# A transformer block with an expert-choice router: logits turned ahead of the shift, lists of maxima copied by ScalarE, second expert's down weights loaded in the router's block

## The reference, cut to what matters

```python
def expert_choice_ffn(h, w_router, w_gate, w_up, w_down):   # h: 1 x 1024 x 1024
    cap = CAPACITY * N // N_EXPERTS                          # 2 * 1024 / 16 = 128
    aff = jax.nn.softmax((h @ w_router).astype(f32), -1)
    gate, idx = lax.top_k(jnp.swapaxes(aff, 1, 2), cap)      # per expert: 128 tokens
    xg = h[bidx, idx]
    g = jnp.einsum('becd,edf->becf', xg, w_gate)
    u = jnp.einsum('becd,edf->becf', xg, w_up)
    y = jnp.einsum('becf,efd->becd', jax.nn.silu(g) * u, w_down) * gate[..., None]
    return jnp.zeros_like(h).at[bidx, idx].add(y)
```

## Time and profile before

| | us |
|---|---|
| median of 3 runs | 3228.96 (3226.36 to 3232.54) |
| the profiled execution, its own time | 3227.27 |
| its span in the trace | 3225.5 |
| router's block, first matmul to the barrier behind it | 778.7 to 827.6 |
| first gathered rows turned on PE | 833.2 |
| steady experts, period of one | about 17.7 |

### The profile page before, as it was taken

The page is one execution under the profiler, slowest core; times in us unless marked ns, Lnnn a source line. Parts: engine busy times, 40 slices in busy tenths (PEclk is TensorE's granted clock), DMA queues, the critical chain, the costliest instruction groups (busy, mean ns, idle before and its releaser), DMA issues. The chain is left out here.

```text
span 3225.5 us, 43947 instructions
## 1 busy us (share of the span) xinstructions
PE 3087.8 (96%) x16276; PEld 2571.9 (80%) x16276; DVE 1702.8 (53%) x2449; ACT 1453.5 (45%) x2464; POOL 1701.3 (53%) x1112
## 2 busy tenths in 40 slices
PE   6989999889899989999999999999999999999998
PEld 4777887857688868788888788888888888888777
DVE  5366623855799786523523644444444444367545
ACT  5156323724577743333301555455455455333443
POOL 2331323044321249877633656556556556688886
PEclk8999999989899989999999999999999999999999
DMA  8230112175899952222522111111111111244553
GB/s 298 56 87 24 54 40 74 45 251 174 324 399 395 356 165 79 79 85 66 175 86 74 39 56 43 47 56 43 47 56 43 46 56 43 89 147 158 183 165 108
DMA packets 340339, 388.11 MB, mean 120 GB/s; under 512 B 29239, under 2 KB 297435, under 8 KB 333860
## 3 DMA queue, kind: packets, MB, share of 16 engines
q1 hardware_dynamic: 328222, 344.39, 31.9%
q0 software_dynamic: 4896, 16.78, 2.1%
q10 hardware_dynamic: 7014, 24.17, 1.9%
HBM read 313.73 MB, written 68.16 MB: 118 GB/s over the span
## 5 line engine op out<-in xcount | busy, mean ns | idle before, releaser
L3011 POOL TENSOR_TENSOR quarter_lo<-quarter_w_sums,quarter_hi 128x512 fp32r<-128x512 f32 x325 | 467.5, 1446 | 246.7 <-ACT quarter_hi L3005 243.8
L3011 POOL TENSOR_TENSOR quarter_lo<-quarter_raw,quarter_hi 128x512 fp32r<-128x512 f32 x244 | 356.3, 1460 | 277.3 <-ACT quarter_hi L3005 270.4
L3101 PE MATMUL odd_z<-odd_t_hi,quarter_hi 128*128 128x512 f32 x876 | 361.9, 413 | 3.9 <-POOL quarter_lo L3011 2.6
L3005 ACT CAST quarter_hi<-quarter_w_sums 128x512 fp32r<-128x512 f32 x325 | 202.3, 622 | 360.1 <-PE first_z L3103 171.1
L3101 PE MATMUL first_z<-odd_t_hi,quarter_hi 128*128 128x512 f32 x868 | 359.4, 414 | 4.0 <-ACT last_rows L3115 2.3
L3103 PE MATMUL odd_z<-odd_t_hi,quarter_lo 128*128 128x512 f32 x876 | 343.1, 392 | 0.0
L3102 PE MATMUL odd_z<-odd_t_lo,quarter_hi 128*128 128x512 f32 x876 | 341.6, 390 | 0.0
L3103 PE MATMUL first_z<-odd_t_hi,quarter_lo 128*128 128x512 f32 x868 | 340.5, 392 | 0.0
L3102 PE MATMUL first_z<-odd_t_lo,quarter_hi 128*128 128x512 f32 x868 | 339.1, 391 | 0.0
L3005 ACT CAST quarter_hi<-quarter_raw 128x512 fp32r<-128x512 f32 x244 | 151.5, 621 | 119.5 <-PE first_z L3103 54.5
L276 POOL TENSOR_TENSOR w_hi<-w_raw,zero_col 128x1024 fp32r<-128x1024 f32 x25 | 49.8, 1994 | 290.5 <-DMA w_raw<-in_w_in 98.2
(11 more groups left out here) (721 smaller groups left out, 7792.5 us busy)
## 6 DMA issues: line engine op xcount, KB each, us to landing
quarter_raw<-in_odd_w_in SPq DMA_DIRECT2D x224, 256.0 KB, 3.4
raw_gate<-in_w_gate SPq DMA_DIRECT2D x16, 2048.0 KB, 16.2
raw_up<-in_w_up SPq DMA_DIRECT2D x16, 2048.0 KB, 15.6
raw_down<-in_w_down SPq DMA_DIRECT2D x16, 2048.0 KB, 15.7
quarter_raw<-in_even_w_in SPq DMA_DIRECT2D x64, 256.0 KB, 3.3
start_w_mod<-in_w_mod SPq DMA_DIRECT2D x11, 1024.0 KB, 10.7
w_raw<-in_w_in SPq DMA_DIRECT2D x16, 512.0 KB, 3.8
mix_w_early<-in_w_mod SPq DMA_DIRECT2D x8, 1024.0 KB, 12.0
```

The lines of the kernel that those rows point to most:

```text
L3005: act.copy(self.home(n)[0][:], self.source(m, i)).then_inc(self.hi_done, 1)
L3011: pool.tensor_tensor(lo[:], self.source(m, i), hi[:].bitcast(F32), ALU.subtract).then_inc(self.split, 1)
L3101: pe.matmul(to, w_hi[:, kt], t_hi[:, kt], start=(begins and kt == 0), stop=False, skip_group_check=True)
```

## The change

Three edits.

1. In PE's list of the router's block the wait for `products_out` and the two transposes of the logits stand ahead of the eight transposes of the shift.
2. DVE's three copies of the lists (L2522 to L2524) go. DVE increments a new semaphore `top_found` after its last round; ACT waits for it at the end of its list, behind `give_part(5)`, and makes the three copies, each incrementing `top_done`; PE waits for 3.
3. The load of `raw["down", 1]` moves from the experts' block to the end of SP's list in the router's block, together with its wait for the four fold stores counted in `fold_stored`. It now increments the semaphore that the load of `raw["up", 1]` increments (renamed `next_loaded`), and ACT waits for 32 of it before it splits either. In the experts' block SP's first DMA is now `last_part`, still behind the two gathers.

```diff
@@ SP, router's block
-                    sp.dma_start(exp_raw["up", 1][:], exp_src["up"][:, 1]).then_inc(next_up_loaded, 16)
+                    sp.dma_start(exp_raw["up", 1][:], exp_src["up"][:, 1]).then_inc(next_loaded, 16)
                     store_fold(5)
+                    sp.wait_ge(fold_stored, 16 * 2 * (FOLDED - 1))
+                    sp.dma_start(exp_raw["down", 1][:], exp_src["down"][:, 1]).then_inc(next_loaded, 16)
                     for u in range(SETS):
                         sp.wait_ge(stored[u], 16 * len(range(u, BLOCKS, SETS)))
                     sp.wait_ge(raw_loaded, 16)
@@ PE, router's block
+                    pe.wait_ge(products_out, 1)
+                    for b in range(2):
+                        ins = pe.transpose(logits[:, b * P:(b + 1) * P], products[:, b * P:(b + 1) * P], ident)
+                    ins.then_inc(logits_done, 1)
                     for kt in range(KT):
                         ins = pe.transpose(shift_t[:, kt // 4, kt % 4 * P:(kt % 4 + 1) * P], mod[:, SH2 + kt, 0:1].to_broadcast([P, P]), ident)
                         if kt % 4 == 3:
                             ins.then_inc(shift_turned, 1)
-                    pe.wait_ge(products_out, 1)
-                    for b in range(2):
-                        ins = pe.transpose(logits[:, b * P:(b + 1) * P], products[:, b * P:(b + 1) * P], ident)
-                    ins.then_inc(logits_done, 1)
...
-                    pe.wait_ge(top_done, 1)
+                    pe.wait_ge(top_done, 3)
@@ ACT, router's block
                     give_part(5)
+                    act.wait_ge(top_found, 1)
+                    act.copy(top_back[:], top[:, ::-1]).then_inc(top_done, 1)
+                    act.copy(top_at_f[:], top_at[:]).then_inc(top_done, 1)
+                    act.copy(top_at_back[:], top_at[:, ::-1]).then_inc(top_done, 1)
@@ DVE, router's block
-                    step(dve.tensor_copy(top_at_f[:], top_at[:]))
-                    step(dve.tensor_copy(top_back[:], top[:, ::-1]))
-                    step(dve.tensor_copy(top_at_back[:], top_at[:, ::-1]))
-                    step.wait()
-                    dve.sem_inc(top_done, 1)
+                    dve.sem_inc(top_found, 1)
@@ experts' block
-                return 16 * (e // 2 + (e % 2 if w == "down" else 0))
+                return 16 * (e // 2)
...
                     for u in range(2):
                         sp.wait_ge(gathered[u], 16)
-                    sp.wait_ge(fold_stored, 16 * 2 * (FOLDED - 1))
-                    sp.dma_start(raw["down", 1][:], exp_src["down"][:, 1]).then_inc(loaded["down", 1], 16)
                     sp.dma_start(last_part[:], even_w[:, :, last_cols]).then_inc(last_part_loaded, 16)
...
-                        if (w, e) == ("up", 1):
-                            act.wait_ge(next_up_loaded, 16)
+                        if (w, e) in (("up", 1), ("down", 1)):
+                            act.wait_ge(next_loaded, 32)
```

More of the change, by code:

```diff
@@ L2224, in build_program @@
         fold_stored = phases.keep("fold_stored")
-        next_up_loaded = phases.keep("exp_next_up_loaded")
+        next_loaded = phases.keep("exp_next_loaded")
         exp_src = {w: A[f"w_{w}"].rearrange("o e (p k) n -> p (o e) k n", p=P) for w in EXP_SHAPES}
@@ L2278, in phase_router @@
             first_fold_stored = sem("fold_first_stored")
+            top_found = sem("route_top_found")
             top_done = sem("route_top_done")
```

## The result

The changed kernel takes 3234.85 us (median of 22 runs, 3231.49 to 3237.72) beside 3229.03 us before (median of 22). The ratio is 1.0018, with a 95% interval of 1.0012 to 1.0025: 5.8 us longer. The forecast was 4.65 us more than before, and a move within 0.2%.

A forecast was written before the change was run, and what follows sets the result against it. PE was taken to bound the experts, so delays to its first work on expert 0 pass through: barrier +2.65 and gather +2.0 give +4.65 us, 3233.6 us on the median of 3228.96; range 3228.5 to 3239.5.

The forecast's parts named there:

- What bounds the kernel: Experts: PE is full, so a shift of its first work on expert 0 goes through to the end.
- the one-for-one rule: Experts: every microsecond at PE's turn of the first gathered rows reaches the end, since PE has no idle time.
- Part 1: Head of router's block: logits ahead of the shift bring the exponential 0.3 us sooner, not 1.1; ACT's shift copies hold it.
- Part 2: End of router's block: list copies on ACT, no longer held by POOL, let DVE finish 3.3 us sooner.
- Part 3, the barrier: End of router's block: SP waits for the last fold store, so the barrier moves back by 2.65 us.
- Part 3, the gather: First gather behind the barrier: the down-weight load in flight beside it costs 2.0 us, bounds 0 to 5.8.
- The page's packet rule: First gather: DMA engines switch queues only after a packet of 9 to 17 descriptors; one load packet ahead costs 1.4 to 2.6 us.
- What the moved load gives back: Experts' block: nobody waited for the down weights there, so loading them earlier gains nothing.
- The gather is starved: Rival, first gather: 9.0 to 10.3 us from issue, contention 4.5 to 5.8, time 3236.1 to 3237.4; chance 0.30.
- SP does not hold the barrier: Rival, end of router's block: fold store lands by 824, barrier 3.3 us sooner, time 3225.7 to 3227.7 or less; chance 0.10.
- No contention: Rival, first gather: it keeps its 4.5 us, total +2.65 us, 3231.6; chance 0.15 including contention under 1.0.

The follow-up runs named there:

- the load moved alone: Kernel before, with only the down-weight load and its fold-store wait moved ahead of the barrier, logits and lists as before: 3234.42 us beside 3227.21, ratio 1.0021.
- the wait alone: Changed kernel with the fold-store wait still ahead of the barrier but the down-weight load back behind the gathers: 3230.68 us beside 3227.21, ratio 1.0010.
- the store put first: Changed kernel with the last fold store issued ahead of expert 1's up weights instead of behind them: 3229.13 us beside 3227.21, ratio 1.0005.
- half of the load: Changed kernel with 1 MB of the down weights issued ahead of the barrier and the other half behind the two gathers: one run, 3233.97 us.

## Why the prediction was right, step by step

- *What bounds the kernel.* Right for a later turn: the load moved alone puts the turn 6.6 us later and the time 7.2 (3234.42 beside 3227.21), the wait alone 2.5 and 3.5, the whole change 6.8 and 5.8, each within the scatter. For a turn that comes sooner the one-for-one rule is not borne out: 4.4 us at the turn were 1.0 in the time, 1.3 to either side.
- *Part 1.* In this profile right in size and reason: the exponential 0.4 us sooner for 0.3, held by the shift's copy. In that the size came out there is luck. The estimate took the shift's transposes at 1.94 us, as in the profile of before; in profiles where the clock fell later they took 1.35 to 1.77, and the exponential came 0.8 to 1.0 us sooner.
- *Part 2.* With part 1 in it, 3.7 us for 3.3. The copies cost what was taken each (0.30, 0.29, 0.29 us), and since they overlap they were through in 0.7 and not in 0.9. One of the merge's additions did wait for POOL, 0.92 us in place of 0.17: it ended at 826.08, POOL at 826.05. I had allowed 0.3 for that. Without this wait the lists would have come 4.5 us sooner.
- *Part 3, the barrier.* Right in mechanism, shown by the wait alone. The term was 2.65 us and measured 3.3. The missing 0.6 is in two places: the store landed 10.6 us after its issue for 10.1, and from the end of SP's issue (832.91) to ACT's first instruction it took 0.66 us where I had taken the 0.30 that follows DVE's last instruction. Together they are 0.86; some 0.25 came back, since part 1 brought the store 0.5 us sooner for 0.3 and SP's step behind the wait was shorter than taken. The landing differs between profiles of the same list (10.1 and 10.1 with the load moved alone and with half of it, 10.5 with the wait alone), so 0.5 of the 3.3 is scatter.
- *Part 3, the gather.* Right in direction, wrong in size: 2.0 us taken, 3.5 measured. The step that failed is "Here the load is beside it for about 3 of these microseconds", and the share of 3/8 made of it. The load was issued 2.06 us ahead of the gather and landed 9.2 us after its issue, at 841.8; the gather's turn began at 842.75. I had let it run at up to 426 GB/s and end by 836. The windows have 197 and 180 GB/s in the first two microseconds and 377 to 442 up to 841:

```profile
833.00:834.00 1.00, 0.00 (x0) 0.00 (x0) 0.37 (x3) 0.43 (x1) 0.00 (x0) 0.50 0.99 197
834.00:835.00 1.00, 0.00 (x0) 0.00 (x0) 0.04 (x1) 1.00 (x1) 0.38 (x1) 0.50 0.57 180
...
841.00:842.00 1.00, 0.00 (x0) 0.00 (x0) 0.00 (x0) 0.00 (x0) 0.00 (x0) 0.50 0.72 295
```

From 833 to 842 that is 3.1 MB, the load and both gathers. A price by the share of time beside each other is the wrong form too: for the whole time it would have given 5.8 us. What the packets show is a first packet 4.3 us after the gather's issue for 1.9, and then two gathers in the stretch of one. The forecast used one gather where two stand in the list.
- *The page's packet rule* (the Trainium skill, DMA: Bandwidth & Descriptors, Queues, rings and completion order) gave, as an estimate, 1.4 to 2.6 us for this term, under the measured 3.5. That estimate took descriptors of 4 KB. The profile's packets of this load are of 16 KB (97 for 1.59 MB), and no run shows after how many of them an engine changes queues, so the rule is neither borne out nor refuted here.
- *What the moved load gives back.* Taken at nothing. From the turn to the end it is 2391.2 us for 2392.3, within the 6 us by which that stretch scatters.
- *The rivals.* "The gather is starved" was meant from 3.8 us on and came close, at 3.5; the gather took 8.1 us, nearer to its row of 9.0 us than to my 6.5. "SP does not hold the barrier" is refuted by the wait alone and by the store put first. "No contention" holds for half the load and not for the whole.
- The sum in the block is 6.8 us for 4.65. The 5.8 us of the medians (the means have 5.8 too, 1.2 to either side) are less than both terms together by 1 us, which is within the scatter. That the time came within 1.2 us of the forecast owes something to that: in the block the forecast was 2.2 us short.

## What to carry to other kernels

A load moved ahead of a block's barrier takes its waits along: before counting what it fills, look when the last of these waits ends against the engine that ends the block now, and at what is queued ahead of the transfer that it waits for. A transfer that the next block needs at once should not find a big one in flight. Half of it issued as early, or the whole one behind the barrier, cost the gather nothing here where the whole one ahead of it cost 3.5 us. And before trimming one engine's share of a block's end, see who becomes the last: 3.7 us of DVE were worth nothing in the changed kernel, and 2.0 to 2.9 at the turn where nobody else waited. Last, profile a kernel twice before reading a difference of 1 us from it.

## What I had not expected of the hardware

- A gather of 128 rows of 4 KB took 4.5 to 4.7 us from issue to PE's turn with no load beside it or with 1 MB issued 2.1 us ahead of it, 5.7 to 6.2 with the tail of 2 MB issued 6.7 us ahead and of a 512 KB store, 7.9 and 8.1 with 2 MB issued 2.1 us ahead, and 9.6 with 4 MB issued 5.3 and 2.4 us ahead.
- Its first packet came 1.9 to 2.1 us after its issue in all of these but the last two groups, where it came 4.3 to 4.4 us after it.
- The barrier opened 0.3 us after DVE's last instruction, and 0.7 us after the end of SP's last DMA issue (0.66 us in the changed kernel, the load moved alone and half of the load). After a wait of SP, with the wait alone, it was 0.4 us: the store landed at 831.5 and ACT went on at 831.90.
- A VectorE addition of 16 columns with both inputs in SBUF took up to 0.92 us while POOL worked, to within 0.03 us of POOL's end, and 0.17 otherwise; those of its neighbours that read PSUM took 0.17 beside POOL.
